# Expert weights in a landing ring of their own, rounded parts and remainders in two rings of five pieces

## The reference

```python
def swiglu(x, w_gate, w_up, w_down):
    return (jax.nn.silu(x @ w_gate) * (x @ w_up)) @ w_down

def moe_sublayer(x, w_router, router_bias, w_gate_e, w_up_e, w_down_e, w_gate_s, w_up_s, w_down_s):
    ...
    scores = jax.nn.sigmoid((xf @ w_router).astype(jnp.float32))
    ...
    _, idx = lax.top_k(jnp.where(emask, choice, -jnp.inf), TOP_K)
    ...
    routed = routed_experts(xf, idx, wts, w_gate_e, w_up_e, w_down_e)
    shared = swiglu(xf, w_gate_s, w_up_s, w_down_s)
    return (shared + routed).reshape(bsz, seq, d)
```

## Time and profile before

| | us |
|---|---|
| median of three runs | 1394.51 |
| lowest and highest of them | 1391.6, 1395.8 |
| the profiled execution | 1394.89 |
| its span, from the first instruction to the last | 1393.2 |
| PE busy | 1314.4 (94%) |
| DVE busy | 897.9 (64%) |
| ACT busy | 709.3 (51%) |
| POOL busy | 399.3 (29%) |
| hardware DMA queue (SP's loads) | 276.64 MB, 54.0% of 16 engines |
| software DMA queue (gathers, scatters) | 33.70 MB, 6.4% of 16 engines |

### The profile page before, as it was taken

The page is one execution under the profiler, slowest core; times in us unless marked ns, Lnnn a source line. Parts: engine busy times, 40 slices in busy tenths (PEclk is TensorE's granted clock), DMA queues, the critical chain, the costliest instruction groups (busy, mean ns, idle before and its releaser), DMA issues.

```text
span 1393.2 us, 15961 instructions
## 1 busy us (share of the span) xinstructions
PE 1314.4 (94%) x6084; PEld 975.8 (70%) x6084; DVE 897.9 (64%) x1167; ACT 709.3 (51%) x863; POOL 399.3 (29%) x266
## 2 busy tenths in 40 slices
PE   7999999999989999988999999999999999999864
PEld 4989886666656776444588777877777777787721
DVE  4001116655665656564398888888888888888848
ACT  4232323333323221011288888887888888887710
POOL 3232312211232343007333323222222222233204
PEclk9999999999989999987999999999999999999978
DMA  4732201211111251531399999999999999999594
GB/s 154 258 105 75 69 20 58 75 39 38 57 38 58 74 198 38 220 113 39 126 382 386 371 377 368 374 371 365 366 368 369 368 369 371 370 368 373 221 380 170
DMA packets 66972, 311.36 MB, mean 223 GB/s; under 512 B 17661, under 2 KB 17789, under 8 KB 40401
## 3 DMA queue, kind: packets, MB, share of 16 engines
q1 hardware_dynamic: 47408, 276.64, 54.0%
q0 software_dynamic: 19488, 33.70, 6.4%
HBM read 305.74 MB, written 42.01 MB: 250 GB/s over the span
## 4 chain that ended last, share of the span: by engine, by line
PE 67%; DMA 22%; ACT 4%; DVE 4%; issue 2%; POOL 0%; POOLq 0%; SPq 0%; DVEq 0%; ACTq 0%
DMA raw<-in_w_gu 20%; PE PS L651 18%; PE PS L895 8%; PE PS L845 4%; PE PS L848 4%; PE PS L759 4%; PE PS L842 4%; PE PS L707 4%; ACT w_hi_e L1113 3%; PE PS L777 3%; PE PS L730 3%; PE PS L827 2%; PE PS L718 2%; PE PS L680 2%; PE PS L679 2%
## 5 line engine op out<-in xcount | busy, mean ns | idle before, releaser
L1430 DVE TENSOR_TENSOR w_lo_e<-raw,w_hi_e 128x2048 fp32r<-128x2048 f32 x192 | 433.8, 2282 | 3.2 <-ACT w_hi_e L1113 3.0
L1113 ACT ACTIVATE w_hi_e<-raw 128x2048 fp32r<-128x2048 f32 x192 | 368.4, 1919 | 111.1 <-DMA raw<-in_w_gu 72.1
L1646 POOL DMA_INDIRECT y_d<-y_slots,tab x64 | 113.7, 1777 | 426.6 <-PE PS L914 283.5
L1600 POOL TENSOR_TENSOR w_lo<-ring,w_hi 128x1024 fp32r<-128x1024 f32 x54 | 128.4, 2378 | 327.2 <-ACT w_hi L1020 327.2
L1273 DVE CUSTOM_DVE_ANT_0 region<-PS,region 128x128 f32<-128x128 f32 (+1 forms) x64 | 30.6, 478 | 183.0 <-PE PS L707 181.0
L845 PE MATMUL PS<-w_hi_e,xs_lo 128*128 128x512 f32 x512 | 144.5, 404 | 0.0
L842 PE MATMUL PS<-w_hi_e,xs_hi 128*128 128x512 f32 x512 | 143.7, 402 | 0.0
L848 PE MATMUL PS<-w_lo_e,xs_hi 128*128 128x512 f32 x512 | 138.7, 393 | 0.0
L1064 ACT ACTIVATE region<-region,nmax 128x128 f32<-128x128 f32 (+3 forms) x80 | 43.6, 545 | 150.1 <-DVE nmax L1273 149.8
L845 PEld LDWEIGHTS PS<-w_hi_e,xs_lo 128*128 128x128 f32 x512 | 91.6, 188 | 33.3 <-DVE xs_lo L1456 15.9
L848 PEld LDWEIGHTS PS<-w_lo_e,xs_hi 128*128 128x128 f32 x512 | 96.1, 188 | 22.3
(11 more groups left out here) (182 smaller groups left out, 2179.6 us busy)
## 6 DMA issues: line engine op xcount, KB each, us to landing
raw<-in_w_gu SPq DMA_DIRECT2D x128, 1024.0 KB, 11.4
raw<-in_w_down_e SPq DMA_DIRECT2D x64, 1024.0 KB, 10.8
ring<-in_w_merge SPq DMA_DIRECT2D x32, 640.0 KB, 3.9
parts<-y_d SPq DMA_DIRECT2D x8, 1536.0 KB, 16.0
ring<-in_w_proj SPq DMA_DIRECT2D x22, 512.0 KB, 3.7
region<-in_w_out SPq DMA_DIRECT2D x1, 4096.0 KB, 14.3
parts<-y_d SPq DMA_DIRECT2D x4, 1024.0 KB, 19.5
bias_d<-bias_rows SPq DMA_DIRECT2D x3, 1280.0 KB, 10.9
```

The source lines that it names most:

```text
L1113: nc.scalar.activation(w_hi_e[b][:, lo:hi], raw[b][:, lo:hi], ACT.Copy).then_inc(made, 1)
L1430: nc.vector.tensor_tensor(w_lo_e[b][:, lo:hi], raw[b][:, lo:hi], w_hi_e[b][:, lo:hi].bitcast(F32), ALU.subtract).then_inc(made, 1)
L1600: nc.gpsimd.tensor_tensor(wl, w, wh.bitcast(F32), ALU.subtract).then_inc(w_lo_made, 1)
L1646: pool.indirect_dma_start(y_d, bass.IndirectOffsetOnAxis(ap=rows, axis=0), y_slots[:, b, :], None, bounds_check=last_row, oob_is_err=False ...
```

## The change

The three pieces of all experts get one numbering, in the order in which they are used (`WEIGHTS`): a0, b0, a1, b1, d0, a2, b2, d1, and so on, 192 in all. They land in a ring of six slots (`LANDED`, `landing(n)`): four in a new tensor `raw`, two of which are the place of x1, and two in the place of x1T, both free once the shared expert and `base` are done. ACT writes the rounded part into a ring of five (`w_hi_e`) and DVE the remainder into another ring of five (`w_lo_e`). SP's `load(n)` waits for the remainder of piece n - 6 to be made; ACT's `high` now also waits until PE has used piece n - 5. The loads of a0 and b0 stand right behind those of the shared weights; a1 and b1 wait for the last gate_up_shared, d0 and a2 for the last `base` and for the stored x1. The shared weights have a place of their own, `raw_s`, which the rings take over later. In memory the twelve piece buffers of before, x1 and x1T (two pieces each) make 16 places of 8 KB a partition; after, the same 16 hold six landed pieces, five rounded parts and five remainders. Nothing else is changed; the branch for more than 128 tokens in one expert follows the new names, and does not run on these inputs.

```diff
--- before.py
+++ after.py
@@ -58,6 +58,11 @@
 STEPS_MOE = QT + N_EXP
 GU = KT * 2 * F
 DN = FT * D
+PIECE = GU // 2
+LANDED = 6
+SPLIT = 5
+LAND_AT = (0, 1, 4, 5, 2, 3)
+SPLIT_AT = (0, 4, 1, 2, 3)
 DVE_RANKS = (5, 6, 7)
 PE_RANKS = (0, 1, 2, 3, 4)
 PIECES = ((5, 8), (0, 3), (3, 5))
@@ -82,6 +87,18 @@
         ("q", BR_B): 772, ("k", BR_B): 1028, ("v", BR_B): 1156,
         ("q", BR_C): 1284, ("k", BR_C): 1540, ("v", BR_C): 1796,
         ("q", BR_D): 2052, ("k", BR_D): 2308, ("v", BR_D): 2564, "gates": 2820}
+
+
+def weight_pieces():
+
+    order = [("a", 0), ("b", 0)]
+    for e in range(1, N_EXP):
+        order += [("a", e), ("b", e), ("d", e - 1)]
+    return order + [("d", N_EXP - 1)]
+
+
+WEIGHTS = weight_pieces()
+PIECE_NO = {x: n for n, x in enumerate(WEIGHTS)}
 
 
 def attention_steps():
@@ -298,20 +315,19 @@
         last = ExitStack()
         parts = last.enter_context(nc.sbuf_tensor("parts", [P, 3, TOP_K, D], F32))
         last.close()
-        raw, w_lo_e, w_hi_e = [None, None], [None, None], [None, None]
-        for b in range(2):
-            landing = ExitStack()
-            raw[b] = landing.enter_context(nc.sbuf_tensor(f"raw{b}", [P, GU + DN], F32))
-            landing.close()
-            w_lo_e[b] = sb(f"w_lo_e{b}", [P, GU + DN], F32R)
-            if b == 0:
-
-                first = ExitStack()
-                first.enter_context(nc.sbuf_tensor("x_nat_from", [P, GU + DN - QT * D], F32))
-                x_nat = first.enter_context(nc.sbuf_tensor("x_nat", [P, QT, D], F32))
-                first.close()
-            w_hi_e[b] = sb(f"w_hi_e{b}", [P, GU + DN], F32R)
-        x1 = sb("x1", [P, QT, D])
+        first = ExitStack()
+        first.enter_context(nc.sbuf_tensor("x_nat_from", [P, KT * D], F32))
+        x_nat = first.enter_context(nc.sbuf_tensor("x_nat", [P, QT, D], F32))
+        raw_s = first.enter_context(nc.sbuf_tensor("raw_s", [P, GU + DN], F32))
+        first.close()
+        w_hi_e = sb("w_hi_e", [P, SPLIT, PIECE], F32R)
+        w_lo_e = sb("w_lo_e", [P, SPLIT, PIECE], F32R)
+        x1_area = ExitStack()
+        x1_area.enter_context(nc.sbuf_tensor("x1_from", [P, 2, PIECE], F32))
+        x1 = x1_area.enter_context(nc.sbuf_tensor("x1", [P, QT, D], F32))
+        x1_area.close()
+        raw = sb("raw", [P, 4, PIECE])
+        raw_ov = raw[:, :, :].rearrange("p a b -> p (a b)")
         h_rows = sb("h_rows", [P, 2, FT, P])
         hT_hi = sb("hT_hi", [P, 2, FT, P], F32R)
         hT_lo = sb("hT_lo", [P, 2, FT, P], F32R)
@@ -332,6 +348,13 @@
         def h_of(b):
 
             return h_rows[:, b, :, :].rearrange("p f n -> p (f n)").rearrange("p (q t) -> p t q", t=FT)
+
+        def landing(n):
+
+            at = LAND_AT[n % LANDED]
+            if at < 4:
+                return raw[:, at, :]
+            return xT[:, :, :].rearrange("p a b -> p (a b)")[:, (at - 4) * PIECE:(at - 3) * PIECE]
 
         def gate_up_of(w):
             return w[:, 0:GU].rearrange("p (c n) -> p c n", c=KT)
...
@@ -533,44 +551,40 @@
 
             PART = GU // 2
 
-            sp.dma_start(raw[1][:, 0:PART], a["w_gu_s"][:, 0:PART]).then_inc(p0_in[1], 16)
-            sp.dma_start(raw[1][:, PART:GU], a["w_gu_s"][:, PART:GU]).then_inc(p1_in[1], 16)
-            sp.dma_start(down_of(raw[1]), a["w_down_s"][0].rearrange("(p t) n -> p t n", p=P)).then_inc(dn_in[1], 16)
-
-            def load_first(e):
-                sp.dma_start(raw[e % 2][:, 0:PART], a["w_gu"][e][:, 0:PART]).then_inc(p0_in[e % 2], 16)
-
-            def load_second(e):
-                sp.dma_start(raw[e % 2][:, PART:GU], a["w_gu"][e][:, PART:GU]).then_inc(p1_in[e % 2], 16)
-
-            def load_down(e):
-                sp.dma_start(down_of(raw[e % 2]), a["w_down_e"][0, e].rearrange("(p t) n -> p t n", p=P))\
-                    .then_inc(dn_in[e % 2], 16)
+            sp.dma_start(raw_s[:, 0:PART], a["w_gu_s"][:, 0:PART]).then_inc(sh_in[0], 16)
+            sp.dma_start(raw_s[:, PART:GU], a["w_gu_s"][:, PART:GU]).then_inc(sh_in[1], 16)
+            sp.dma_start(down_of(raw_s), a["w_down_s"][0].rearrange("(p t) n -> p t n", p=P)).then_inc(sh_in[2], 16)
+
+            def load(n):
+                what, e = WEIGHTS[n]
+                if n in (2, 3):
+                    sp.wait_ge(gu_b, QT)
+                elif n in (4, 5):
+                    sp.wait_ge(based, 2 * QT)
+                    sp.wait_ge(x1_stored, 16 * QT)
+                elif n >= LANDED:
+                    sp.wait_ge(lo_made, n - LANDED + 1)
+                if what == "d":
+                    weights = a["w_down_e"][0, e].rearrange("(p t) n -> p (t n)", p=P)
+                else:
+                    weights = a["w_gu"][e][:, 0:PART] if what == "a" else a["w_gu"][e][:, PART:GU]
+                sp.dma_start(landing(n), weights).then_inc(piece_in[n % LANDED], 16)
 
             def store_x1(t):
                 sp.wait_ge(x1_made, t + 1)
                 sp.dma_start(x1_d[t * P:(t + 1) * P, :], x1[:, t, :]).then_inc(x1_stored, 16)
 
+            load(0)
+            load(1)
             store_x1(0)
             store_x1(1)
-            sp.wait_ge(mix_done, QT)
-            load_first(0)
-            load_second(0)
-            load_down(0)
             store_x1(2)
             store_x1(3)
+            sp.wait_ge(x1_made, QT)
             sp.dma_start(ln[:, 0, :], bass.AP(a["ln2_g"].tensor, 0, [[0, P], [1, D]])).then_inc(ln2_in, 16)
             sp.dma_start(ln[:, 1, :], bass.AP(a["ln2_b"].tensor, 0, [[0, P], [1, D]])).then_inc(ln2_in, 16)
-            for e in range(1, N_EXP):
-                sp.wait_ge(gu_a, e + QT - 1)
-                load_first(e)
-                sp.wait_ge(gu_b, e + QT - 1)
-                load_second(e)
-                if e >= 2:
-                    sp.wait_ge(y_done, e + QT - 2)
-                    load_down(e - 1)
-            sp.wait_ge(y_done, N_EXP + QT - 2)
-            load_down(N_EXP - 1)
+            for n in range(2, len(WEIGHTS)):
+                load(n)
 
 
             sp.wait_ge(most_made, 1)
...
@@ -830,22 +844,24 @@
 
             def gate_up(e, part):
 
-                b, s = e % 2, e + QT
-                wh, wl = gate_up_of(w_hi_e[b]), gate_up_of(w_lo_e[b])
-                made_hi, made_lo = ((p0_hi, p0_lo), (p1_hi, p1_lo))[part]
-                cs = range(part * KT // 2, (part + 1) * KT // 2)
+                b, s, n = e % 2, e + QT, PIECE_NO["ab"[part], e]
+                at = SPLIT_AT[n % SPLIT]
+                wh = w_hi_e[:, at, :].rearrange("p (c n) -> p c n", c=KT // 2)
+                wl = w_lo_e[:, at, :].rearrange("p (c n) -> p c n", c=KT // 2)
+                c0 = part * KT // 2
+                cs = range(c0, c0 + KT // 2)
                 pe.wait_ge(h_made, s - 1)
                 pe.wait_ge(xs_hi_made, e + 1)
-                pe.wait_ge(made_hi, e + 1)
+                pe.wait_ge(hi_made, n + 1)
                 to = PS[:, G_BANK + s % 2, :]
                 for c in cs:
-                    nc.tensor.matmul(to, xs_hi[:, b, c, :], wh[:, c, :], start=(c == 0), stop=False)
+                    nc.tensor.matmul(to, xs_hi[:, b, c, :], wh[:, c - c0, :], start=(c == 0), stop=False)
                 pe.wait_ge(xs_lo_made, e + 1)
                 for c in cs:
-                    nc.tensor.matmul(to, xs_lo[:, b, c, :], wh[:, c, :], start=False, stop=False)
-                pe.wait_ge(made_lo, e + 1)
+                    nc.tensor.matmul(to, xs_lo[:, b, c, :], wh[:, c - c0, :], start=False, stop=False)
+                pe.wait_ge(lo_made, n + 1)
                 for c in cs:
-                    mm = nc.tensor.matmul(to, xs_hi[:, b, c, :], wl[:, c, :], start=False, stop=(c == KT - 1))
+                    mm = nc.tensor.matmul(to, xs_hi[:, b, c, :], wl[:, c - c0, :], start=False, stop=(c == KT - 1))
                 mm.then_inc((gu_a, gu_b)[part], 1)
 
             def turn_h(s):
...
@@ -874,16 +890,18 @@
                 for half in range(FT):
                     for n in range(2):
                         mm = nc.tensor.matmul(PS[:, bank + n, :], hT[:, t % 2, half, :],
-                                              down_of(raw[1])[:, half, n * 512:(n + 1) * 512],
+                                              down_of(raw_s)[:, half, n * 512:(n + 1) * 512],
                                               start=(half == 0), stop=(half == 1))
                 mm.then_inc(y_done, 1)
 
             def down(e):
 
-                b, s = e % 2, e + QT
-                wh, wl = down_of(w_hi_e[b]), down_of(w_lo_e[b])
+                s, piece = e + QT, PIECE_NO["d", e]
+                at = SPLIT_AT[piece % SPLIT]
+                wh = w_hi_e[:, at, :].rearrange("p (t n) -> p t n", t=FT)
+                wl = w_lo_e[:, at, :].rearrange("p (t n) -> p t n", t=FT)
                 pe.wait_ge(hT_made, s + 1)
-                pe.wait_ge(dn_hi, e + 1)
+                pe.wait_ge(hi_made, piece + 1)
                 if e == 0:
                     pe.wait_ge(based, 2 * QT)
                 else:
...
```

(50 more changed lines are left out.)

23 lines of the change are left out of this document (7 added, 16 removed).

## The result

| | before | after |
|---|---|---|
| median of 6 runs each, us | 1395.4 (1391.6 to 1397.45) | 1404.27 (1401.72 to 1405.81) |
| ratio, 95% interval | | 1.0065 [1.0052, 1.0078] |
| profiled execution, us (its span) | 1394.89 (1393.2) | 1404.86 (1403.2) |

The prediction was 1391.9 us with a range of 1384 to 1398. Its sign was wrong: a slower kernel had been given a chance of 0.08.

The account below looks back on a forecast made before the run. The bound was taken to be a closed DMA-PE loop over two buffers, with row-carrying DMA engines saturated. Terms -1 (removed waits), -2 (start) and 0 elsewhere took 1394.89 us to 1391.9 us, range 1384 to 1398.

Parts of the forecast that it names:

- the sum for the loaded half: Expert stretch: engines carrying gathered and scattered rows need 7.40 + 2.40 = 9.80 us per expert.
- Step 1: Expert loads: SP's waits for PE removed, up to 4.7 pieces under way; -5.3 to 0 us, taken as -1.
- Step 2: Start of the expert loads: stream 3.0 to 1.3 us ahead despite one more piece; taken as -2 us.
- Steps 3 and 4: ScalarE's added waits before rounding, and the same instructions at other addresses: 0 us each.
- Step 5: End, after the last gate-up rounding: the closing chain moves with a63, early d63 gains nothing; 0 us.
- Rival A: Expert stretch: DMA has headroom, experts run at PE's 9.34 us; -33 us, 1361 to 1386 us; chance 0.13.
- Rival B: Expert stretch: deeper queue delays gathers and PE waits for rows; slower, 0.3 us each would give 1410 us; chance 0.07.
- the signs: What the profile after should show in the experts and at their start if the forecast of 1391.9 us was right.
- the landing (14 to 16): Expert stretch: a weight piece's time from issue to landing grows from 11.4 to 14 to 16 us.
- b2 before 701.5: Start: the second gate-up piece of expert 2 has landed by 701.5 us; before, it was awaited until 702.83.
- the rate (370): Expert stretch: the DMA rate stays at 370 GB/s.
- the period (9.8 to 9.9): Expert stretch: the period of down, per expert, stays between 9.8 and 9.9 us.

Follow-up runs that it names:

- e1: Kernel before, with each expert's rows spread over both halves of the partitions, so that all 16 DMA engines carry them: 1360.47 us, 0.9758.
- e7: Kernel before with spread rows and part of the work left out (two remainder products, seven of eight chunks of x remainders): 1344.32 us, 0.9636.
- e8: Changed kernel with spread rows and the same work left out as in e7: 1344.71 us, 0.9638.
- e12: e8 with the down load's old wait for PE put back, as in e5: 1344.91 us, 0.9657.
- e4: Changed kernel, but each load also waits until PE has used piece n - 6, the wait of the kernel before: 1394.12 us, 0.9998.
- e5: Changed kernel with the old wait for PE put back for down pieces alone: 1428.72 us, 1.0241.
- e6: Changed kernel with the old wait for PE put back for gate-up pieces alone: 1411.37 us, 1.0116.
- e11: Kernel before, with scatter and gather held back until the running expert's second gate-up product: 1411.86 us, 1.0124.
- e17: Kernel before, gather issued first and the scatter alone held back until the running expert's second gate-up product: 1407.47 us, 1.0078.

## Why the prediction was wrong, point by point

- The bound was read rightly: a closed loop over a saturated DMA, with the engines that carry the rows as its floor. When the rows were spread, the floor went and PE's 9.34 us took its place (e1). That the sum for the loaded half, 9.80 us, met the measured 9.90 so closely has some luck in it: the same sum gives 8.60 us for an even load, and e7, e8 and e12 took 9.1 to 9.2.
- Step 1 is the step that failed. Its depth was right: 4.7 pieces under way were forecast, and 15.3 us of landing over a cadence of 10.09 / 3 = 3.36 us are 4.6. Its price was given as -5.3 to 0 us, "with saturated engines the cadence stays". It did not stay. It went from 3.30 to 3.36 us per piece, which is +11.8 us. I had treated the rate of a saturated engine as a constant and only allowed it to rise, and so cut off the slower end without a row that excluded it. The runs showed that this rate depends on when loads and scatters are issued (346 to 370 GB/s for the same bytes per expert), and that the wait removed had held a good timing.
- Step 2, the start, was right for the DMA: b2 had landed when ScalarE began to round it at 700.43, against 702.83 before. PE got less of it, -0.4 us at down(0) and -0.9 at down(1), for -2 forecast, since its period there was already its floor (710.39 - 701.05 = 9.34 us).
- Steps 3 and 4, the waits added to ScalarE and the new places, cost 0 as forecast: e4 has them all and runs at 0.9998.
- Step 5: the end moved with a63 and gained 1.0 us beyond that, for 0 forecast.
- Rival A is refuted for this change (no gain), though its reading of the share had a point: 0.99 stood beside engines with time to spare. That room is opened by spreading the rows, not by asking sooner.
- Rival B had the sign but not the mechanism. Gathers land after 11.0 us instead of 10.8, and PE does not wait for them.
- Of the signs, the share (0.99), the landing (14 to 16), SP's wait for DVE, ScalarE's waits for landings and b2 before 701.5 came true; the rate (370) and the period (9.8 to 9.9) did not, and these two carried the result.

What is shown: the loss is a slower DMA, it is there at 3.6 pieces under way as at 4.6, the new places and the added waits have no part in it, and the way of issuing that costs most (e5) costs nothing clear of noise once the rows lie on both halves (e12). Both the gaps between the loads (e6) and the place of the scatter among them (e11, e17) move the time. What stays open: which of the two costs the changed kernel its 9 us, since it differs from the kernel before in both, and no run puts one back and leaves the other as it is; whether the deeper queue has a part of its own in it; and what inside the loaded half makes a piece take longer.

## What to carry to other kernels

A wait that a saturated loop seems not to need may still be setting the rhythm of its DMA. Price its removal on both sides of zero, even when the queue stays full either way, and look where the other transfers will then start among the loads. Before deepening a queue, ask whether all DMA engines have the same load: rows that fill the low partitions first put the whole transfer on half of them, and spreading the slots was worth 34 to 35 us here where the deeper ring was worth -9.

## What the runs showed of the hardware

- With the same bytes per expert and three or more pieces always under way, the DMA moved 369 GB/s in one kernel, 362 in another, 356 when the scatter started 3 us later and the gather 4, and 346 when two loads were issued 0.4 us apart and then none for 7.6 us.
- With the rows spread over both halves of the partitions the same kernels moved 392 GB/s and, with less work on PE, 403 to 407. There three ways of issuing came to 1344.3, 1344.7 and 1344.9 us, two of which lay 24 us apart with the rows on one half.
- The share of busy DMA engines was 0.97 to 1.01 in all of these except e5, from 356 to 407 GB/s. It did not tell the fast rates from the slow ones.
- With the rows on partitions 0 to 63, eight of the 16 engines report their part of a 1 MiB load 5.0 to 5.8 us after its issue, whether 3.4 or 4.6 pieces are under way, and the last one after 11.2 and 15.4 us. With the rows spread the last one reports after 7.8 us (e1).
